# RWKV scan of a four-mixer Trainium2 kernel: X and Y in one product by tokens, U beside Y, turned blocks on ScalarE's transfer queue

## What is computed

```
def _rwkv_step(S, inp):
    r, w, kk, kka, kt, v = inp
    sk = jnp.einsum('bhij,bhj->bhi', S, kk)
    S = S * w[:, :, None, :] - sk[..., None] * kka[:, :, None, :] + v[..., None] * kt[:, :, None, :]
    return S, jnp.einsum('bhij,bhj->bhi', S, r)
...
        S_f, y_f = _rwkv_scan(S0[0], (r, w[0], kk, kk * a[0], kt[0], v), False)
        S_b, y_b = _rwkv_scan(S0[1], (r, w[1], kk, kk * a[1], kt[1], v), True)
```

## Time and profile before

| | |
|---|---|
| median of three runs | 3853.27 us |
| profiled execution, its own time | 3850.02 us |
| its span (first to last instruction) | 3848.3 us |
| mean granted TensorE clock | 0.942 of full speed |
| TensorE matmul busy | 3417.3 us (89%) |
| VectorE, ScalarE, GpSimd busy | 1747.0, 1178.4, 552.4 us |
| chain that ended last, TensorE's share | 70% |

### The profile page before, as it was taken

The page is one execution under the profiler, slowest core; times in us unless marked ns, Lnnn a source line. Parts: engine busy times, 40 slices in busy tenths (PEclk is TensorE's granted clock), DMA queues, the critical chain, the costliest instruction groups (busy, mean ns, idle before and its releaser), DMA issues.

```text
span 3848.3 us, 65362 instructions
## 1 busy us (share of the span) xinstructions
PE 3417.3 (89%) x28861; PEld 2311.7 (60%) x28861; DVE 1747.0 (45%) x2909; ACT 1178.4 (31%) x2057; POOL 552.4 (14%) x754
## 2 busy tenths in 40 slices
PE   6999989999999898745776899898989999989998
PEld 5777776343343766545664443236757888756887
DVE  4324641121222654963356222126855546855454
ACT  3225722111111565921112111003253234334233
POOL 2220120000000210048513000001102210101210
PEclk8999998999999998867888899999999999989999
DMA  6531147989886352987533999993203313212322
GB/s 246 184 107 52 61 167 266 375 313 370 317 313 262 124 182 98 313 223 183 145 102 133 344 415 420 419 420 133 88 22 118 113 62 107 70 54 99 101 86 77
DMA packets 314859, 739.32 MB, mean 192 GB/s; under 512 B 68248, under 2 KB 148896, under 8 KB 265424
## 3 DMA queue, kind: packets, MB, share of 16 engines
q1 hardware_dynamic: 302480, 697.18, 49.7%
q0 software_dynamic: 12096, 37.96, 3.1%
HBM read 673.19 MB, written 61.89 MB: 191 GB/s over the span
## 4 chain that ended last, share of the span: by engine, by line
PE 70%; DVE 10%; DMA 8%; ACT 5%; issue 2%; SPq 2%; POOL 0%; DVEq 0%; POOLq 0%; ACTq 0%
PE ps L62 66%; DMA raw<-in_moe_w_dram 6%; PE ps L66 4%; SPq L120 2%; DVE mx L75 1%; DVE mx L102 1%; DVE mrn L99 1%; DVE b L75 1%; DVE cr L75 1%; DMA Tb<-ot 1%; DVE o L75 1%; DVE o L81 0%; ACT cr L72 0%; DMA c<-in_w_ple_gate_dram 0%; ACT lw L72 0%
## 5 line engine op out<-in xcount | busy, mean ns | idle before, releaser
L62 PE MATMUL ps<-raw,xinT 128*64 128x512 f32 (+1 forms) x4096 | 591.6, 492 | 32.8 <-DMA raw<-in_moe_w_dram 23.6
L62 PEld LDWEIGHTS ps<-raw,xinT 128*64 128x64 f32 (+1 forms) x4096 | 196.0, 123 | 401.4 <-issue 288.1
L62 PE MATMUL ps<-wp,hp 128*128 128x512 f32 x1024 | 314.1, 393 | 8.6 <-ACT wp L72 8.6
L62 PE MATMUL ps<-cr,oTr 128*128 128x512 f32 (+2 forms) x1024 | 255.6, 382 | 3.5 <-ACT oTr L72 3.1
L75 DVE TENSOR_TENSOR mx<-mx,ps 128x512 f32<-128x512 f32 (+1 forms) x196 | 127.3, 663 | 234.6 <-PE ps L62 133.3
L62 PEld LDWEIGHTS ps<-wp,hp 128*128 128x128 f32 x1024 | 193.8, 190 | 49.0 <-issue 8.8
L62 PEld LDWEIGHTS ps<-cr,oTr 128*128 128x128 f32 x1024 | 187.6, 188 | 38.9 <-ACT oTr L72 3.6
L62 PE MATMUL ps<-wp,hTr 128*128 128x512 f32 x512 | 194.4, 389 | 0.0
L62 PE MATMUL ps<-raw,hidT 128*64 128x512 f32 x768 | 177.9, 602 | 3.2 <-DMA raw<-in_moe_w_dram 3.2
L62 PE MATMUL ps<-ar,naxh 128*128 128x512 f32 x576 | 147.4, 406 | 19.0 <-DVE ar L75 8.8
L75 DVE TENSOR_TENSOR wp<-c,wp 128x1536 fp32r<-128x1536 f32 x32 | 60.6, 1894 | 180.7 <-ACT wp L72 180.7
(11 more groups left out here) (535 smaller groups left out, 6332.4 us busy)
## 6 DMA issues: line engine op xcount, KB each, us to landing
raw<-in_moe_w_dram SPq DMA_DIRECT2D x384, 1024.0 KB, 7.7
c<-in_w_in_dram SPq DMA_DIRECT2D x28, 2048.0 KB, 9.3
mx<-in_ada_w_dram SPq DMA_DIRECT2D x14, 2048.0 KB, 8.0
raw<-in_ada_w_dram SPq DMA_DIRECT2D x8, 2048.0 KB, 13.5
a<-in_na_w_qkv_dram SPq DMA_DIRECT2D x6, 2048.0 KB, 7.9
c<-in_w_branch_dram SPq DMA_DIRECT2D x16, 512.0 KB, 5.9
c<-in_w_out_dram SPq DMA_DIRECT2D x4, 2048.0 KB, 10.8
c<-in_w_ple_gate_dram SPq DMA_DIRECT2D x4, 2048.0 KB, 7.9
```

What stands on the lines that cost most here:

```text
L62: return self.e.matmul(out, lhsT, rhs, start=start, stop=stop, skip_group_check=True) if self.e is not None else self
```

## The change

- **X and Y in one product.** Operands are laid out anew: `ar` holds, for each pair, columns r | a | a | r of the two halves, `bk` b | k | k | b, so that `gram` makes G with 128 weight columns in half as many matmuls, and x1 and x2 give X and the two first parts of Y at once, for 128 output partitions: X in one half, Y by tokens in the other, in two banks per direction parity. `VU` holds V in one half of the partitions and U in the other, so that the state update is one product of height 128 (`s`); v is gone.
- **U beside Y.** The last part of Y (from U) of the half before is issued alternately with U of this half, on complementary tiles. x1 and this pair each have a wait of TensorE for itself in the middle, since two row tiles must not write to one bank.
- **Evictions.** X by direction (four instructions), U by direction (two). Y is copied by ScalarE in rounds 4 to 7, added by VectorE from round 8, each half on its own. The readout's first transposes are gone.
- **Turned blocks.** `store(n)` and `load_t(r)` stand on ScalarE's queue; a load is four DMAs instead of two. In odd rounds the next block's last rows (24 to 31) are solved by VectorE at the round's start, then stored and loaded in the same round. GpSimd solves rows up to 23 (of block 1 only 11 to 23).
- **Loads.** `load` has 12 DMAs in a latent round instead of 8 (r and b by halves, 256-byte runs), `load_m` 12 instead of 4 (V comes by rounds, with time-major b and k), and `load_m(r+1)` stands ahead of `load(r+2)`. The readout's V (2 MB) is fetched at the end of round 2, behind 2 MB of output weights. The first three sets of squares are issued ahead of everything.
- **Banks.** `take` gives the bank that was taken or released longest ago.
- Masks, `main`, `own`, `Q`, `X`, `bon` and the scratch of the solve are put into other tiles.

The core of the diff:

```diff
-        while self.next % 8 in self.held.values():
-            self.next += 1
-        b = self.next % 8
-        self.next += 1
+        b = next(x for x in self.queue if x not in self.held.values())
+        self.last(b)
...
-    load(0)
-    load_m(0)
-    load(1)
-    load_m(1)
+    for r in range(2):
+        load(r)
+        load_m(r)
+    rows(0, 1, 31)
+    store(0)
+    load_t(0)
...
+    for n in range(1, 6):
+        rows(n, 1, LATE - 1)
...
     for r in range(12):
-        more = r + 1 < 12
+        more, n = r + 1 < 12, (r + 1) // 2
+        whole = more and r % 2
+        if more and not whole:
+            load_t(r + 1)
+        if more and r:
+            load_m(r + 1)
         if r + 2 < 12:
             load(r + 2)
-        if more:
-            load_t(r + 1)
-        some(3 if r else 8)
+        if whole:
+            rows(n, LATE, 31)
         recur(r, 0, 'x2')
-        recur(r, 0, 'y1')
-        recur(r, 0, 'y2')
-        one(r)
-        recur(r, 0, 'u')
-        recur(r, 0, 'v')
         if more:
             gram(r + 1, 0)
-            gram(r + 1, 1)
-        some(4 if r else 8)
+        recur(r, 0, 'u')
+        if whole:
+            store(n)
+        one(r)
+        recur(r, 1, 'x1')
         recur(r, 0, 's')
         one(r)
-        recur(r, 0, 'y3')
-        recur(r, 1, 'x1')
+        if more:
+            gram(r + 1, 1)
+        one(r)
+        recur(r, 1, 'x2')
+        if whole:
+            load_t(r + 1)
+            refill(n)
         if more:
             gram(r + 1, 2)
+            blocks(r + 1)
+        one(r)
+        recur(r, 1, 'u')
+        if more:
             gram(r + 1, 3)
-            blocks(r + 1)
-        some(3 if r else 8)
+        recur(r, 1, 's')
         one(r)
-        recur(r, 1, 'x2')
-        recur(r, 1, 'y2')
         if more:
             level(r + 1, 0)
-        one(r)
-        some(3 if r else 7)
-        recur(r, 1, 'u')
-        recur(r, 1, 'v')
-        if more:
+            recur(r + 1, 0, 'x1')
             level(r + 1, 1)
-        recur(r, 1, 's')
-        recur(r, 1, 'y3')
-        some(3)
-        one(r)
-        if more:
-            recur(r + 1, 0, 'x1')
-        if r + 2 < 12:
-            load_m(r + 2)
         if r in (2, 9):
             rows_in(r)
-
-
-def rw_scan(P, I, ring, F, Tm, Ad, Td, vd, Lm, acc, V, sa, sT, R):
+    recur(12, 0, 'u')
...
+                for c in range(2):
+                    cols = pair(c) if lat(r) else keys(c)
+                    for p in range(2):
+                        k = 2 * g + i
+                        ins = e.matmul(P.psum[:, banks[p], i * 256 + cols.start:i * 256 + cols.stop], bk(r, z)[half(p), k, pair(c)], ar(r, z)[half(p), k, cols],
+                                       (i, c) == (0, 0), True)
...
+        def products_y(r, i, k, turn):
+            for z in range(2):
+                c, p = cut(z, i), z ^ turn
+                h = 2 * k + p
+                yield e.matmul(P.psum[half(c), P.banks.place.get(('x', r, i, p), 0), bank_of(z, k)], G(r, z)[half(1 - c), h, reads(c)],
+                               VU(r, z)[half(1 - c), i, sh(h)], False, True)
...
+                for turn in range(2):
+                    if turn:
+                        e.wait_ge(*P.pe.at('x1a', r, i))
+                    for k in range(4):
+                        for z in range(2):
+                            c, p = cut(z, i), z ^ turn
+                            h = 2 * k + p
+                            out = P.psum[:, banks[p], bank_of(z, k)] if lat(r) else P.psum[half(1 - c), banks[p], bank_of(z, k)]
+                            ins = e.matmul(out, G(r, z)[half(c), h, pair(c) if lat(r) else keys(c)], VU(r, z)[half(c), i, sh(h)],
+                                           k == 0 and (turn == 0 or not lat(r)), False)
+                    ins.then_inc(*P.pe.inc('x1' if turn else 'x1a', r, i))
...
-                            ins = e.matmul(P.psum[c, banks[p], sh(k)], ar(r, z)[half(p), 0, k, c], state(r, z)[half(p), k, :], False, True)
+                            c = cut(z, i)
+                            out = P.psum[:, banks[p], bank_of(z, k)] if lat(r) else P.psum[half(1 - c), banks[p], bank_of(z, k)]
+                            ins = e.matmul(out, ar(r, z)[half(p), k, pair(c) if lat(r) else keys(c)], state(r, z)[half(p), k, :], False, True)
                 ins.then_inc(*P.pe.inc('x', r, i))
...
+                for turn in range(2):
+                    if there:
+                        e.wait_ge(*(P.pe.at('ya', q, j) if turn else P.pe.at('x', q, j)))
...
+                        us = products_u(r, i, 4 * turn + k) if here else ()
+                        ys = products_y(q, j, k, turn) if there else ()
+                        for a, b in itertools.zip_longest(us, ys):
+                            if a is not None:
+                                of_u = a
+                            if b is not None:
+                                of_y = b
+                    if here and turn:
+                        of_u.then_inc(*P.pe.inc('u', r, i))
+                    if there:
+                        of_y.then_inc(*P.pe.inc('y' if turn else 'ya', q, j))
...
+                    e.wait_ge(*P.act.at('u', r, i, z))
+                    c = cut(z, i)
+                    for k in range(4):
...
+                            h = 2 * k + p
+                            ins = e.matmul(P.psum[half(p), b, bank_of(z, k)], tm(r, z)[:, c, sh(h)], VU(r, z)[:, i, sh(h)], (z, k) == (0, 0), True)
...
+                for z in range(2):
+                    o = half(1 - cut(z, i))
+                    for p in range(2):
+                        e.activation(X[o].rearrange("p (k e i) -> p e k i", e=2, i=64)[:, p],
+                                     P.bank('x', r, i, p)[o, 256 * z:256 * z + 256].rearrange("p (k i) -> p k i", i=64), ACT.Copy).then_inc(*P.act.inc())
...
+        def store(n):
+            e.wait_ge(*P.dve.at('row', n, 31))
+            for z in range(2):
+                e.dma_start(Td[z][ORDER[z][n]].rearrange("h (d n) -> (h d) n", d=4), Tv_of(n)[64 * z:64 * z + 64]).then_inc(*s_td[n].inc())
+            s_td[n].name('td', n)
+
+        def load_t(r):
+            e.wait_ge(*s_td[step(r)].at('td', step(r)))
+            if r:
+                e.wait_ge(*P.pe.at('z5', r - 1))
+                e.wait_ge(*P.dve.at('blocks', r - 1))
+            for z in range(2):
+                src = Td[z][ORDER[z][step(r)]][group(r) * 8:group(r) * 8 + 8].rearrange("h (p s) -> p h s", p=128)
+                for c in range(2):
+                    e.dma_start(dt_[half(1 - c), z, 0, :].rearrange("p (h s) -> p h s", h=8), src[half(c)]).then_inc(*s_dt.inc())
+            s_dt.name('dt', r)
...
+            if n == 0 or i >= LATE or (n == 1 and i <= FIRST):
+                if n and i == LATE:
+                    e.wait_ge(*P.pool.at('row', n, i - 1))
+                solve_row(e, P.dve, n, i)
...
+                src = {nm: F[nm, z][f, chunk(r, z) * 128:chunk(r, z) * 128 + 128].rearrange("(k p) t -> p k t", p=128) for nm in 'arbk'}
+                e.dma_start(ar(r, z)[:, :, 64:192], src['a']).then_inc(*s_ar[r % 3].inc())
+                e.dma_start(bk(r, z)[:, :, 64:192], src['k']).then_inc(*s_bk[r % 2].inc())
+                for c in range(2):
+                    if lat(r):
+                        e.dma_start(ar(r, z)[:, :, reads(c)], src['r'][:, :, half(c)]).then_inc(*s_ar[r % 3].inc())
+                    e.dma_start(bk(r, z)[:, :, reads(c)], src['b'][:, :, half(c)]).then_inc(*s_bk[r % 2].inc())
...
+                for c in range(2):
+                    t = slice(chunk(r, z) * 128 + 64 * c, chunk(r, z) * 128 + 64 * c + 64)
+                    e.dma_start(VU(r, z)[half(c), cut(z, c), :], vd[t, f]).then_inc(*s_vu[r % 2].inc())
+                    e.dma_start(tm(r, z)[half(c), c, :], Tm['b', z][t, f]).then_inc(*s_tm[r % 2].inc())
+                    e.dma_start(tm(r, z)[half(1 - c), c, :], Tm['k', z][t, f]).then_inc(*s_tm[r % 2].inc())
```

More of the change, by code:

```diff
@@ L142, in take, with last @@
         return b, [s.at(*event) for s, *event in before]
+    def last(self, b):
+        self.queue.remove(b)
+        self.queue.append(b)
     def release(self, key):
-        del self.held[key]
+        self.last(self.held.pop(key))
 class Ring:
@@ L2684, in act @@
             e.wait_ge(*P.dve.at('ycentred', c))
+            e.wait_ge(*P.dve.at('row', 5, 31))
             if c != 1:
@@ L2757, in rows, with rw_scan_order @@
         self.s_g.name('readout')
[L2760 to L2763 removed]
+def rw_scan_order(const, load, load_m, load_t, gram, blocks, level, recur, solve, store, refill, read, rows_in):
     reads = iter(READ)
[L2766 to L2768 removed]
     def one(r):
@@ L2992, in recur @@
                 ins.then_inc(*P.pe.inc('x', r, i))
-                for p in range(2):
-                    P.banks.release(('x', r, i, p))
-            if what == 'y1' and lat(r):
-                banks = []
-                for c in range(2):
```

(22 more changed lines are left out.)

354 lines of the change are left out of this document (129 added, 225 removed).

## The result

The changed kernel takes 3911.84 us (median of 4 runs, 3908.91 to 3919.16) against 3852.07 for the kernel before: ratio 1.0167, 95% interval 1.0149 to 1.0184. It is 60 us slower where I had forecast 13 faster; 3911.84 lies outside my range, beyond every rival I had priced.

A forecast was written before the change was run, and what follows sets the result against it. The scan was taken as bound by a chain of short products, evictions and waits, not by TensorE. Latent rounds -13.7, context rounds -9.5 and issue waits +10 gave -13 us: 3837, or 3840 as a median; range 3814 to 3876.

The forecast's parts named there:

- the latent rounds at -13.7 us: Scan rounds 4 to 9: predicted to take 153.1 us against 166.8 before.
- issue waits: Scan: TensorE waiting for its instructions, 41.4 us before; 10 kept on the path, added as +10, bounds 3 and 28.
- the context rounds at -9.5: Scan rounds 0 to 3: predicted 93.6 us against 103.1, where SyncE's queue is bypassed for turned blocks.
- nothing for the rest: Work before round 0, the last two rounds and GpSimd's rows: 0 us; last two rounds bounded -3 and +4.
- Wide products: X and Y in one product with 128 weight columns: x2 2.1 us, x1 2.3, bounds 1.4 and 3.8.
- don't pair: Rival: 64-row halves with 128 columns don't run side by side, each X product 3.8 us: +41, 3880; chance 0.08.
- TensorE's work hardly shrinks: Latent rounds: wide x1 and x2 cost more, y1, y2 and v go; what shrinks is phases and instructions.
- Odd rounds: Odd latent rounds: 26.2 us each, with the turned load issued at 13.8 and the last landing at 18.55.
- each free when asked for: New PSUM bank order: four rotating banks beside four held, each free when asked for, followed through one round.
- Late features: Rival: Gram waits for feature loads delayed on SyncE's queue; three late us in ten rounds give 3870; chance 0.22.
- More won: Rival: issue waits go, odd rounds' turned load is hidden, wide products partly at 1.4 us: 3815; chance 0.20.
- no effect: Rival: the turned load only moves its wait from SyncE to ScalarE and VectorE: 3850, the forecast's own upper edge.

The follow-up runs named there:

- e16: Changed kernel plus 32 unread products in front of level 0 in rounds 1, 3, 5, 7 and 9: 3927.91 us, ratio 1.0209.
- e7: Changed kernel with X alone on 64 weight columns and Y of the latent tokens left out: 3880.60 us, ratio 1.008.
- e6: Changed kernel with the turned block's loads issued ahead of the second half's X eviction in odd rounds: 3899.60 us, ratio 1.0132.
- e3: Changed kernel with rows 24 to 31 of every block but the first solved on GpSimd instead of VectorE: 3914.51 us, ratio 1.0165.
- e4: Changed kernel with the readout's 2 MB of V fetched behind round 6 instead of round 2: 3904.61 us, ratio 1.0144.
- e8: Changed kernel with r and b fetched in whole rows of 128 tokens, 16 feature transfers per latent round instead of 24: 3920.59 us, ratio 1.0186.
- e9: Kernel before with turned blocks stored and loaded on ScalarE's queue, two transfers each, old banks: 3846.00 us, ratio 1.0003.
- e13: Kernel before with turned blocks on ScalarE's queue, but block 0's store and first load left on SyncE's: 3846.44 us, ratio 1.0.
- e15: Changed kernel plus 16 unread products in front of level 0 in rounds 1, 3, 5, 7 and 9: 3920.60 us, ratio 1.0179.
- e17: Changed kernel with old banks in the merge, V behind round 6, turned load ahead of X's eviction, and e15's 16 products: 3868.51 us, ratio 1.0057.

## Why the prediction was wrong, point by point

The sum had three parts: the latent rounds at -13.7 us and 10 for the issue waits, the context rounds at -9.5, and nothing for the rest. Between the traces they came out at +18.8, +13.2 and +26.7 (rounds 4 to 9; rounds 0 to 3; start of round 0 -5.0, behind round 10 +13.1, up to the merge -0.7, merge +19.3). Each part failed by a step of its own.

**Wide products: right at full clock, sized for the wrong clock.** I took 2.1 us for x2 and 2.3 for x1; measured 2.00 and 2.28, s 1.15 as predicted. Both row halves do run side by side (in round 5 the records of x2 start in pairs 0.007 us apart, a pair every 0.112 us); the rival "don't pair" falls. But my latent rounds left the clock where the earlier trace rows had it, 0.90. It was 0.74, and at half clock the two cost 3.68 and 4.01. This is the step that failed in the latent rounds, and with it "TensorE's work hardly shrinks" turned from harmless to dear. An estimate: 149.08 us busy at 0.74 is 110 us of work at full speed, against 117.37 x 0.90 = 106 before, the same work as I had said (e16, less 22 us of filling, gives 110 too); at 0.90 it would have been 123 us busy, 26 less. Not all of that lies on the path. What a low clock costs a round can be read across the eleven kernels with wide products: of their even rounds 4, 6 and 8, the twelve with a clock of 0.78 or more took 27.2 us in the mean (25.3 to 29.4), the seven below 0.70 took 29.8 (29.2 to 31.3). That is a relation between rows; no run set the clock alone. With narrow X rounds 4 to 9 are 22.6 us shorter (e7), and their clock is 0.78. After round 10 it is 0.53, where it had been 0.89. I had put the part behind round 10 at 0, at most +4; it was +13.1, and with narrow X 12 of them are gone (64.2 us for 76.1), so they too are the width of X.

**Odd rounds: landing mis-sized.** Predicted 26.2 us; measured 31.0, 33.5 and 37.6. The load is issued where I put it (13.9 us into round 5; 13.8 predicted), but the four issues take 2.9 us for 1.8, and the last lands 5.55 us later for 3.4, at 21.7 instead of 18.55. What follows takes 9.3 us for 7.65, at half clock. This round stood at a clock of 0.88, so the clock alone does not explain it. e6 shows what the place in ScalarE's queue was worth, 9 us in six rounds.

**Even rounds: 25.3 us in round 4 for 23.7, then 29.6 and 28.6** with the clock at 0.67 and 0.74; e7, with narrow X, gives 23.2 to 25.2. At a clock of 0.85, in round 4, the price was 1.6 us too low; the rest goes with the clock.

**Context rounds: wrong sign, +13.2 for -9.5.** The step that failed is when the turned load goes out and lands in the odd ones: I had 11.75 and 16.5 us into the round; it went out at 17.4 (round 1) and 13.4 (round 3), and had landed at 26.5 and 27.9. Two causes are shown by runs, the third only by its rows: rows 24 to 31 on VectorE in front of the mask, 16 instructions at 0.6 us where I had 0.37 at most (e3: 7 us in round 1); V in round 3, for which I had 4 us (e4: 8; e8 wins as much there with fewer, longer transfers and V in place); and the transfers of block 1 and 2, which the new queue freed from SyncE only for them to wait in the DMA engines (6.85 and 12.42 us to land, against 2.9 to 4.5). Round 2 stays unexplained: 25.5 us where I had 21.3, with a clock of 0.62 for 0.77 in the kernel before. (For the clock of the context rounds I wrote 0.74; the row says 0.73.) That SyncE's queue held the load up was right (e9: 12.4 us shorter rounds), that bypassing it would pay was not: e9 and e13 leave the time where it was.

**Banks: "each free when asked for" was wrong inside the scan, and "nothing for the rest" wrong outside.** I followed the new order through one round of the scan alone. x1 of the second half needs none of the masks it waited 5.48 us for in round 1, only a bank, by its operands (argued from the code, no run isolates it). The larger error is that the order is global: +19.9 us in the merge, -7 in the expert products. Neither stage was in my working at all, though the diff changed a function that all of them call.

**Issue waits: right, and better.** I kept 10 of 41.4 us; 1.3 are left. It did not help, since TensorE then waits for the turned block.

**Late features: refuted.** One wait of 1.3 us in the whole scan. The Trainium skill, "DMA: Bandwidth & Descriptors", Specifications, wants at least 512 bytes for line rate. Whole rows did lower the DMA share, 0.65 to 0.57, but not the time of the whole (e8).

**More won, no effect:** neither came. GpSimd's rows were no bound, as said: with eight more of them (e3) the store went out no later in rounds 7 and 9.

What stays open: why the clock fell. In rounds 4 to 9 it is 0.90 with TensorE busy 70% of the time (before), 0.74 at 80% (after), 0.75 at 87% (e15), 0.82 at 88% (e16), 0.78 at 65% (e7). The busy share does not order these. The wait in front of level 0 may have a part in it (e16, e17), but e6 has hardly any of it and 0.73, and e7 has it whole (6.5 us) and 0.78. With narrow X the clock in the even rounds 4 and 6 was 0.85 and 0.81, for 0.85 and 0.67 in the kernel after.

## What to carry to other kernels

A change to a shared allocator has to be costed at every stage that calls it, not where it was written for: here one function moved -7 us at one place and +20 at another, and using it only where it helps gave 0.3%. Replacing many small products by fewer wide ones keeps TensorE's work and raises its busy time if the granted clock falls; put the clock into the sum as a term with both levels. Filling idle time can go with a higher clock and still win nothing, if the filling takes as long as it gives back. Before moving work onto a second engine or queue, price each instruction with its neighbour running, and look at what else is in the DMA engines at that time.

## What the hardware showed that I had not expected

- VectorE's tensor_tensor with both inputs in SBUF took 0.68 us for 31 columns beside GpSimd's rows (round 1) and 0.19 with GpSimd idle (round 5), a factor of 3.6; at 112 columns 0.61 and 0.27.
- Wide products on half the rows (64 by 128 weights, 64 columns) pair across row halves: 2.00 us for 32 records at full clock, 62 ns each, against 117.5 for full-height ones.
- In the kernel after a 64 KB turned load landed in 2.4 to 3.4 us at the start of the even rounds and in 5.5 to 12.4 us in the odd ones, where the DMA share was 0.66, 1.02 and 0.75 (rounds 1, 3 and 5). Issued 11.7 us earlier in the kernel before (e9, round 3), it landed only 2.7 us earlier.
- The granted clock of a chain of products went from 0.90 to 0.74 though fewer products were issued, filling 3.8 us of idle time in every odd round left it there (0.75, e15), and filling 7.4 us, the whole wait, went with 0.82 and the same time (e16).
